# One stream of expert rows across the steps, and an attention step's queries and bias rows loaded first

## The reference

```python
sh1, sc1, g1, sh2, sc2, g2 = modulation(cond, p['w_ada'], p['b_ada'])
outs, state = token_mixer(x * (1 + sc1) + sh1, p)       # 12 attention heads and a gated MLP
x = layer_norm(ALPHA * x + g1 * merge_groups(outs, ...), p['ln1_g'], p['ln1_b'])
x = layer_norm(ALPHA * x + g2 * peer_ffn(x * (1 + sc2) + sh2, p), p['ln2_g'], p['ln2_b'])
...
def one_block(xb):                                      # peer_ffn, a block of 128 tokens
    q = (xb @ p['peer_w_q']).reshape(128, 8, 2, 128)
    s = jnp.einsum('thpd,pnd->thpn', q, p['peer_sub_keys'])
    ...                                                 # two top-16, then the top 16 of their sums
    act = jax.nn.gelu(jnp.einsum('thkd,td->thk', p['peer_u'][eid], xb))
    return jnp.einsum('thk,thkd->td', gate * act, p['peer_v'][eid])
```

## Time and profile before

| | us |
|---|---|
| median of 3 runs | 5283.75 |
| lowest and highest | 5277.81, 5296.46 |
| profiled execution, time | 5288.38 |
| profiled execution, span | 5286.6 |

### The profile page before, as it was taken

The page is one execution under the profiler, slowest core; times in us unless marked ns, Lnnn a source line. Parts: engine busy times, 40 slices in busy tenths (PEclk is TensorE's granted clock), DMA queues, the critical chain, the costliest instruction groups (busy, mean ns, idle before and its releaser), DMA issues. The chain is left out here.

```text
span 5286.6 us, 34528 instructions
## 1 busy us (share of the span) xinstructions
PE 3032.0 (57%) x9560; PEld 1575.4 (30%) x9560; DVE 3434.8 (65%) x6877; ACT 633.4 (12%) x1577; POOL 2815.9 (53%) x2837
## 2 busy tenths in 40 slices
PE   7638766366356546547554676645554663565354
PEld 1423344134133223311232333423332331332111
DVE  1255467677776866773568555667686677769775
ACT  0101121120121111000110001111111201211000
POOL 1116645366466646644654564445664664665675
PEclk8768868678678767778777786777776886787676
DMA  8447778789899988989896878769898998998998
GB/s 337 159 184 247 250 281 339 292 334 390 309 346 356 352 328 329 393 313 368 325 361 259 307 242 305 286 259 348 343 377 316 337 391 305 339 358 345 355 404 322
DMA packets 439839, 1690.09 MB, mean 320 GB/s; under 512 B 53120, under 2 KB 66496, under 8 KB 427568
## 3 DMA queue, kind: packets, MB, share of 16 engines
q0 software_dynamic: 370528, 1353.39, 67.7%
q1 hardware_dynamic: 69120, 334.49, 16.4%
HBM read 1660.02 MB, written 33.95 MB: 320 GB/s over the span
## 5 line engine op out<-in xcount | busy, mean ns | idle before, releaser
L571 PE MATMUL ps<-ring,diag 128*128 128x512 f32 x1456 | 875.8, 747 | 844.8 <-ACT diag L545 748.7
L502 POOL DMA_INDIRECT ring<-in_peer_u,eid_s x728 | 785.8, 1079 | 596.0 <-DVE dots L603 360.0
L502 POOL DMA_INDIRECT ring<-in_peer_v,eid_s x728 | 737.8, 1013 | 487.1 <-PE ps L571 217.7
L502 POOL DMA_INDIRECT W<-in_peer_v,eid_s x552 | 570.4, 1033 | 349.7 <-issue 125.9
L571 PE MATMUL ps<-W,diag 128*128 128x512 f32 x1104 | 618.8, 698 | 234.2 <-DMA W<-in_peer_v,eid_s 164.6
L603 DVE CUSTOM_DVE_ANT_0 ring<-ring,ps 128x1024 f32<-128x1024 f32 x552 | 658.4, 1217 | 142.4 <-DMA ring<-in_peer_u,eid_s 139.5
L603 DVE CUSTOM_DVE_ANT_0 W<-W,ps 128x1024 f32<-128x1024 f32 x552 | 655.6, 1217 | 102.0 <-DMA W<-in_peer_u,eid_s 100.7
L571 PEld LDWEIGHTS ps<-ring,diag 128*128 128x128 f32 x1456 | 320.7, 235 | 1296.8 <-issue 1126.0
L502 POOL DMA_INDIRECT W<-in_peer_u,eid_s x552 | 540.5, 979 | 292.6 <-DVE dots L603 130.1
L613 DVE SCALAR_TENSOR_TENSOR acc<-ring,wsel,acc 128x1024 f32<-128x1024 f32 x364 | 474.2, 1303 | 99.1 <-DMA ring<-in_peer_v,eid_s 69.5
L613 DVE SCALAR_TENSOR_TENSOR acc<-W,wsel,acc 128x1024 f32<-128x1024 f32 x276 | 354.8, 1286 | 50.0 <-DMA W<-in_peer_v,eid_s 24.7
(11 more groups left out here) (212 smaller groups left out, 3311.5 us busy)
## 6 DMA issues: line engine op xcount, KB each, us to landing
W<-in_w_q SPq DMA_DIRECT2D x40, 2048.0 KB
W<-in_w_ada SPq DMA_DIRECT2D x24, 2048.0 KB
W<-in_w_out SPq DMA_DIRECT2D x10, 4096.0 KB, 30.5
W<-in_w_in SPq DMA_DIRECT2D x16, 2048.0 KB, 10.1
ring<-in_peer_u,eid_s POOLq DMA_INDIRECT x728, 6.7
ring<-in_peer_v,eid_s POOLq DMA_INDIRECT x728, 6.3
toep<-mod_rows SPq DMA_DIRECT2D x20, 512.0 KB, 8.7
aux<-mod_rows SPq DMA_DIRECT2D x19, 512.0 KB, 5.7
```

The source lines that it names most:

```text
L502: pool.indirect_dma_start(slot(E, r), None, a["peer_u"] if kind == "u" else a["peer_v"], bass.IndirectOffsetOnAxis(ap=eid_s[:, h % 4, k:k ...
L571: last = pe.matmul(acc_ps[:, c * 512:(c + 1) * 512], diag[:, (E.by_pe[r] - 1) % DIAGS, :], slot(E, r)[:, c * 512:(c + 1) * 512], start=Fal ...
```

## The change

The `Experts` objects give way to one `Stream` of all 2560 rows and a `Slice` of it for each step. Semaphores that count rows are no longer cleared between steps, so gathers run on over a barrier:

- Towards the end of a step POOL also issues the gathers of the next step's first rows, up to 8 (before input and modulation steps, and from one to the first latent attention) or 16, as far as these rows are routed. It issues each after the last user of its tile, the step's own last rows included, before it goes to the barrier.
- The last 16 rows of a block (v rows) are left over to the next step, where attention steps take them first, 16 of 256 shares, ahead of the first score. The first latent attention has 112 rows for 128; the modulation step of layer 1 80 for 64; the experts-only step 272 for 256. Steps of whole blocks keep 256.
- In attention steps SP loads the expert numbers, queries, `toep` and `band`, then the experts' input and gates, then the four tiles of the ended sum.
- A head has 8 shares for 9, a stage of the routing's top-16 work 8 for 9, and DVE's order in a head is: next scores, 5 of 8 shares, this head's result, the other 3.
- The first latent attention and the context attention alternate u and v rows too. Expert numbers and gates have two buffers; the staging copies on POOL go. The first PE row of a block starts its sum (`start=opens`), the first DVE row sets `acc`; the clearing and the extra matmuls go.
- `last_sum` becomes a generator that runs one piece after each row of the next block, and POOL's operation for it comes 16 rows on.

```diff
+LEAD = TOPK
+TAIL_SHARE = 16
...
-    8: (9, (8, 16, 24, 40), 8, 9),
+    8: (8, (8, 16, 24, 40), 8, 8),
...
+    def order(self, parts):
+        order, first = [], 0
+        for heads, turn in parts:
+            one = [("u", first + h, k) for h in range(heads) for k in range(TOPK)]
+            two = [("v", first + h, k) for h in range(heads) for k in range(TOPK)]
+            order += one[:LEAD]
+            one = one[LEAD:]
+            while two:
+                order += one[:turn] + two[:turn]
+                one, two = one[turn:], two[turn:]
+            first += heads
+        assert first == PH and len(order) == self.JOB
+        return order
...
+    def place(self):
+        self.slot, self.landed, self.prev = [], [], []
+        user, count = [-1] * DEEP, [0] * DEEP
+        for i, S in enumerate(self.slices):
+            from_shallow = i == 0 or not self.slices[i - 1].deep
+            for r in range(S.start, S.end):
+                wide = S.deep and not (from_shallow and r < S.start + RING)
+                at = min(range(DEEP if wide else RING), key=lambda n: (user[n], n))
+                self.slot.append(at)
+                self.prev.append(user[at])
+                user[at] = r
+                count[at] += 16
+                self.landed.append(count[at])
...
+        self.limit = min(self.end + ahead, stream.JOB * routed)
...
+        FULL = [(PH, 1)]
+        BESIDE_INPUTS = [(1, 1)] * NLAT + [(PH - NLAT, 1)]
+        BESIDE_CONTEXT = [(2, TOPK), (1, 1), (PH - 3, 1)]
...
-        def experts_sync(sp, E):
-            if E is not None and E.begin:
-                sp.dma_start(eid_e[:, :], of_block(eid_dram, E.block)).then_inc(ids_in, 16)
-                if E.ended is not None:
-                    last_sum_in(sp, E.layer, E.ended, ended_tiles)
-                sp.dma_start(x2e[:, :], of_block(x2_dram, E.block)).then_inc(e_in, 16)
-                sp.dma_start(gates_e[:, :], of_block(gate_dram, E.block)).then_inc(e_in, 16)
+        def experts_sync(sp, S):
+            experts_sync_ids(sp, S)
+            experts_sync_rest(sp, S)
+        def experts_sync_ids(sp, S):
+            if S is not None and S.begins is not None:
+                j = S.begins
+                sp.dma_start(eid_e[:, j % 2, :], of_block(eid_dram, JOBS[j][1])).then_inc(ids_in, 16)
+        def experts_sync_rest(sp, S):
+            if S is not None and S.begins is not None:
+                j = S.begins
+                sp.dma_start(x2e[:, :], of_block(x2_dram, JOBS[j][1])).then_inc(e_in, 16)
+                sp.dma_start(gates_e[:, j % 2, :], of_block(gate_dram, JOBS[j][1])).then_inc(e_in, 16)
+            if S is not None and S.ended is not None and not S.at_end:
+                last_sum_in(sp, *JOBS[S.ended], ended_tiles)
...
-        def last_sum(dve, tiles):
+        def last_sum(dve, j, tiles):
             link = chain(dve, end_chain)
-            link(dve.tensor_tensor(acc[:, :], acc[:, :], acc_ps, ALU.add))
+            r = stream.last(j)
+            dve.wait_ge(used_dve, by_dve[r])
+            dve.wait_ge(used_pe, by_pe[r])
+            ins = dve.tensor_tensor(acc[:, :], acc[:, :], acc_ps, ALU.add)
+            ins.then_inc(acc_free, 1)
+            dve.wait_ge(acc_free, j + 1)
+            yield
+            yield
             dve.wait_ge(end_in, 64)
             link(dve.tensor_tensor(acc[:, :], acc[:, :], tiles[1], ALU.mult))
+            yield
             link(dve.scalar_tensor_tensor(acc[:, :], tiles[0], ALPHA, acc[:, :], ALU.mult, ALU.add))
-            layer_norm(link, dve, acc[:, :], tiles[2], tiles[3], tiles[0], st12e, mve, vee[:, :], rstde[:, :],
-                       end_var, end_rstd, 1).then_inc(end_done, 1)
+            yield
+            link(dve.bn_stats(st12e[:, 0, :], acc[:, 0:512]))
+            link(dve.bn_stats(st12e[:, 1, :], acc[:, 512:1024]))
+            link(dve.bn_aggr(mve[:, :], st12e[:, :, :].rearrange("p a n -> p (a n)")))
+            dve.tensor_scalar_add(vee[:, :], mve[:, 1:2], EPS).then_inc(end_var, 1)
+            for _ in range(8):
+                yield
+            dve.wait_ge(end_rstd, 1)
+            link(dve.tensor_scalar(acc[:, :], acc[:, :], mve[:, 0:1], rstde[:, :], ALU.subtract, ALU.mult))
+            yield
+            link(dve.tensor_tensor(acc[:, :], acc[:, :], tiles[2], ALU.mult))
+            yield
+            dve.tensor_tensor(tiles[0], acc[:, :], tiles[3], ALU.add).then_inc(end_done, 1)
+        RSTD_AT = 16
...
+            pow_due = [S.ended is not None and not S.at_end]
+            def rows(share):
+                t = S.target(share)
+                while pool_at[0] < S.limit and stream.prev[pool_at[0]] < t:
+                    r = pool_at[0]
+                    j, kind, h, k = rows_of[r]
+                    if r == stream.first(j):
+                        pool.wait_ge(ids_in, 16 * (j + 1))
+                    p = stream.prev[r]
+                    if p >= 0:
+                        _, q, _, qk = rows_of[p]
+                        if on_pe(q, qk):
+                            pool.wait_ge(used_pe, by_pe[p])
                         else:
-                            pool.wait_ge(used_dve, E.by_dve[r - E.slots])
+                            pool.wait_ge(used_dve, by_dve[p])
                     pool.indirect_dma_start(
-                        slot(E, r), None, a["peer_u"] if kind == "u" else a["peer_v"],
-                        bass.IndirectOffsetOnAxis(ap=eid_s[:, h % 4, k:k + 1], axis=0)).then_inc(gath[r % E.slots], 16)
-                    at[0] += 1
-            gather_until(E.slots)
-            def rows(share):
-                gather_until(E.target(share) + E.slots)
+                        row_tile(r), None, a["peer_u"] if kind == "u" else a["peer_v"],
+                        bass.IndirectOffsetOnAxis(ap=eid_e[:, j % 2, h * TOPK + k:h * TOPK + k + 1], axis=0)).then_inc(gath[stream.slot[r]], 16)
+                    pool_at[0] += 1
+                    if pow_due[0] and pool_at[0] == stream.last(S.ended) + 1 + RSTD_AT:
+                        pow_due[0] = False
+                        last_sum_rstd(pool)
...
+                        opens = h == 0 and k == 0
+                        if opens and j:
+                            pe.wait_ge(acc_free, j)
...
+                        elif h == 0 and k == 1:
+                            if ending[0] is not None:
+                                for _ in ending[0]:
+                                    pass
+                                ending[0] = None
+                                dve.wait_ge(end_done, 1)
+                            dve.tensor_scalar_mul(acc[:, :], row_tile(r), wsel[:, g % 2, k:k + 1]).then_inc(used_dve, 1)
...
+                    if S.ended is not None and r == stream.last(S.ended) and not S.at_end:
+                        ending[0] = last_sum(dve, S.ended, ended_tiles)
+                    if ending[0] is not None:
+                        next(ending[0], None)
...
-            A_END = NH * HEAD_SHARE
+            HEAD_SHARE, tail, q_share, route_share = SHARES[shares]
+            A_START = TAIL_SHARE if after_tail else 0
+            A_END = A_START + NH * HEAD_SHARE
             TAIL = [A_END + n for n in tail]
-            HEAD_MID = HEAD_SHARE // 2
+            HEAD_MID = HEAD_SHARE * 2 // 3
             ROUTE = [TAIL[-1] + min(i + 1, 4) * q_share + max(i - 3, 0) * route_share for i in range(12)]
...
-                    experts_sync(sp, E)
+                    experts_sync_ids(sp, E)
...
                     if not context:
                         lay(toep[:, :, :], toep_dram[L, :, :].rearrange("p (h n) -> p h n", h=H)[:, :, ds((2 * NLAT - 2 * b) * GRID_W, lat)], x_loaded)
                         lay(band[:, :], a["c_band"][:, ds(NLAT * P - b * P, lat)], x_loaded)
+                    experts_sync_rest(sp, E)
                     lay(ob[:, 0:GW], spill_dram[ds(b, 1), :, SP_A:SP_C].rearrange("b p n -> (b p) n"), loaded2)
                     lay(W[:, 0:KD * D], a["w_out"][L, :, :], loaded2)
...
+                    rows(A_START)
                     pe.wait_ge(loaded, 32)
                     score(0)
                     for i in range(NH):
                         if i + 1 < NH:
                             score(i + 1)
-                        rows(i * HEAD_SHARE)
+                        rows(A_START + i * HEAD_SHARE)
                         pe.wait_ge(exp_done, i + 1)
...
                     for i in range(NH):
-                        if i == 1:
-                            rows(HEAD_MID)
-                            experts_gpsimd_ended(pool, E)
-                        rows(i * HEAD_SHARE)
+                        rows(A_START + i * HEAD_SHARE)
...
+                    rows(A_START)
                     if not context:
                         dve.wait_ge(x_loaded, 32)
                     negate_max(0)
                     for i in range(NH):
                         if i + 1 < NH:
                             negate_max(i + 1)
```

(93 more changed lines are left out.)

276 lines of the change are left out of this document (126 added, 150 removed).

## The result

| | before | after |
|---|---|---|
| median of 5 runs, us | 5283.75 | 5248.85 |
| lowest and highest | 5277.81, 5296.46 | 5244.62, 5256.99 |
| profiled span | 5286.6 | 5255.2 |

The ratio is 0.9926 (95% interval 0.9913 to 0.9938): 35 us faster, where 195 were forecast. 5248.85 lies above the predicted range.

What follows compares the result with a forecast made beforehand. No engine is near full; whole-block attention was taken as a DVE and PE chain. Terms -156 (whole-block), -22 (first latent), -18 (input), +9 (modulation), -8 (context) make -195 from 5286.6: forecast 5089 us, range 4960 to 5235.

Steps and rivals of the forecast that it cites:

- The failed step: End of a whole-block step: one more gather issued by POOL before the barrier, 1.3 us, up to 2.3.
- Input steps: Nine input steps with experts: POOL's shorter start saves 3 us, gathers at the end cost 1; -18 us in all.
- The -3 for POOL's shorter start: Input steps: 12 gathers instead of 20 before POOL's first other operation, for which DVE waits 3.72 us; -3 each.
- Whole-block steps: Six steps, -26 us each, -156 in all: start and attention gain 32, the other stages lose 6.
- Attention: Attention stage of a whole-block step: 96 rows for 108, 125 us of DVE work plus 29.5 of waits, 154.5 us.
- Rival A: Whole-block attention held only to DMA's 152 us from the barrier: -47 a step, 4963 us; chance 0.17 (4940 to 5030).
- The middle stages: Whole-block step: projection and queries cost 5 us (less row lead), top-16 gains 5 (fewer shares).
- Modulation: Modulation step of layer 1: DMA-bound, 16 more rows make 79.8 MB at 415 GB/s; +9 us (0 to +20).
- Context attention: Context attention of layer 1: same 160 rows, 8 already there at the start; -8 us (0 to -20).
- Experts only: Experts-only step: 16 rows more, 16 prefetched, same 256 gathers in a DMA-bound step; 0 us (-5 to +3).
- D: Barriers: tiles come free so late that DMA idles as now; about -12 a whole step, 5173; with B 0.25.
- C: Attention heads: PE's loop gets longer as ended-sum pieces delay it, slower kernel from 15.6 us a head; chance 0.06.

Runs made afterwards that it cites:

- after_no_drain: The kernel after, but with step ends that compare semaphores only and don't wait for GpSimd's gathers in flight: 5135.0 us, ratio 0.9716.
- The square: Four kernels: old head order without stream 5288 us, new order 5128; with stream and rows ahead into deep steps, old order 5301, new 5139.
- ahead_deep_only: The kernel after, with rows gathered ahead only into steps that asked for 16 and none into the others: 5138.6 us, ratio 0.9734.
- ahead_none: The kernel after with no row gathered ahead over any step's end; left-over rows, load order and shares stay: 5247.7 us, ratio 0.9933.

## Why the prediction was wrong

- **The barrier.** The failed step is the price of the step's end: "POOL must issue one more gather after the last row before it may go to the barrier: 1.3 us" and, for input steps, "+1 for the gathers at the end". One issue was counted, and the landing put at nothing without a reason. The runs show that POOL issues five gathers after DVE's last row, and that from the last issue to the next step 9.4 us pass, 0.9 with a step end that compares semaphores only. From the ids' store to the next step 7.9 us in before were to become 14 (+6); it took 26.2, and 17.8 with the open step end. In before no step ends with gathers in flight: its last one is issued 20 us ahead of the next step in whole-block steps, 7 to 8 in input steps. But the page of before has the median from a gather's issue to its landing:

```profile
ring<-in_peer_v,eid_s POOLq DMA_INDIRECT x728, 6.3
```

18 ends at that price would have been 113 us, an estimate; opening the step ends gave 114, an agreement that is partly chance, as a wait holds more than the landing.
- **Input steps**, nine: forecast -18, measured +107. This is 125 of the 160 us missed: the closed step end holds 53 of it (`after_no_drain`), the other rows ahead do the rest. The -3 for POOL's shorter start didn't show either: in the step from 447.3 DVE still waits 3.5 us for that operation, since POOL gets no free tile before DVE's first row, and DVE waits for the input.
- **Whole-block steps**: -26 each forecast; -19 to -24 with 16 rows ahead, -31 for the one that ends with 8. Start 19.3 us for 18.5 forecast; its last wait is 6.7 us for PE's left-over rows, as the working had it. That it is right to 1 us is luck: "two rows cost 3.43 us at 1.2 GHz" misreads. The four matmuls shown there are one expert row (the page has 2560 of them for 640 diagonals of ACT), so 8 rows at that clock are 27 us, not 14. They took 17, as the granted clock rose after PE had worked for some 6 us:

```profile
1434.00:1437.00 3.00, 3.00 (x4) 1.01 (x3) 2.79 (x3) 0.40 (x1) 0.68 (x1) 0.50 0.66 212
1440.00:1444.00 4.00, 4.00 (x11) 1.81 (x10) 2.08 (x2) 1.34 (x3) 3.08 (x4) 1.00 1.02 377
```

  Attention 144 us for 154.5: DVE is busy 123.7 for 125, and its waits are 20.4 us for 29.5, since those for scores went wholly. Start and attention took 163.4 us for 173. Rival A's floor, 152 us of DMA from the barrier on, was not reached, though DMA did hold 411 GB/s in the attention stage. The middle stages +4 for 0. Against the forecast, start and attention came out 10 us better a step, the middle stages 4 worse and the end 12 worse.
- **Where the gain comes from.** The prediction credits it to the left-over rows and the filled tiles first and to the order in a head as cover. The square says the reverse: the order alone makes 160 of it. For the two first latent attentions it makes 14 and 18 us where 8 were allowed.
- **Modulation**: +32 for +9. The rows' part held (8 us), though the step ran at 357 GB/s and not at the 415 of the working, which no row shows. Missed was SP's queue: the wait for the ended result was priced at 0 since "nobody needs" what stands behind it before the projection; true in attention steps, but in the modulation step `w_ada` stands behind it.
- **Context attention** (-12 for -8) right: the 8 rows ahead are worth 8.5 us (325.6 without, `ahead_deep_only`). **Experts only** -9 for 0: the rows ahead are worth 20 us to it (`ahead_none`), where the working took the step as bound by DMA.
- **Rivals.** None was this. D came nearest (a pause at the barrier), but for another reason, tiles that come free late; POOL's pause is there, 14.9 us without a gather, and DMA does work in the first part of it. C didn't show: heads took 12.0 us.
- **The signs named beforehand** worked: "at most 5 us between POOL's gathers at a barrier" and "input steps that don't shorten" both pointed at the place.

## What to carry to other kernels

Before work is put in flight over a barrier, find out what the barrier waits for; if the trace has no case of it, put the landing time of the queue, from the profile's list of transfers, into the sum. When a large change has a small reordering in it, price and try the reordering alone: here one moved line of rows between a result and the next scores was worth more than the rest of the rewrite. For every wait that moves later, look at each kind of step in which it stands and at what its queue has behind it.

## What the runs showed of the hardware

- At this kernel's ordinary step end all engines wait until POOL's gathers have landed, though no engine's program names them: 9.4 us after the last issue with three to four rows' worth of them still queued (6.0 to 9.9 over 18 ends), 0.9 us with semaphores alone. Where none is in flight the two kinds of end don't differ (ratio 0.9997).
- The DMA engines stood empty for 4.3 of these 9.4 us; what fills them is open.
- From the issue of a 0.52 MB load on SP's queue to PE's first matmul with it, 3.7 us passed with no gathers in flight and 7.3 with them (3.2 to 4.9 and 6.7 to 7.8 over the input steps that load no weights); the barrier's wait had hidden this.
- The wait leaves every engine's busy time as it was; only the time from the last instruction of a step to the next step's first transfer shows it.
